# The first iteration of each FFN reordered by chunks of columns, with the norm of later chunks behind it

## Chip, cores, metric

One NeuronCore of a Trainium2 chip. The metric is the device time in microseconds of one execution; lower is better.

## What is computed

One inference step of a two-layer decoder for 1024 prompt tokens and 8 x 4 sample tokens, model width 1024, all in float32. Each layer is a token mixer followed by a SwiGLU FFN; the change touches only the FFNs.

```python
def rmsnorm(x, g):
    xf = xf * lax.rsqrt(jnp.mean(xf * xf, axis=-1, keepdims=True) + RMS_EPS)
    return xf.astype(x.dtype) * g
def swiglu(h, w_in, w_out):
    g, u = jnp.split(h @ w_in, 2, axis=-1)
    return (jax.nn.silu(g) * u) @ w_out
# per sub-layer, shift, scale and gate from the conditioning vector
h = rmsnorm(x, norm_g[i, 1]) * (1 + sc) + sh
x = x + gt * swiglu(h, ffn_w_in[i], ffn_w_out[i])
```

D_FF is 2816. The 32 sample tokens have a shift, scale and gate for each sequence of the batch.

## The kernel before

The activations lie transposed in SBUF: `xT` has 8 tiles (KD) of 128 features by 1056 tokens (T). The tokens are cut into NCH = 3 chunks of CH = 352 columns; the last one ends with the 32 sample tokens. A float32 product is made of three matmuls: every operand is split into a rounded high half and a low half, and hi x hi, lo x hi and hi x lo are added in PSUM.

`ffn_phase` (L639) runs N = 11 iterations. Each takes two blocks of 128 gate and up columns (`a` = 0 and 1) and the two matching blocks of the down weights (`a` = 2). The weights of an iteration are three loads of 1 MB into the two halves of `raw` (blocks 0 and 2 share half 0). ACT writes the high half (`split_hi`, L687), POOL the low one (`split_lo`, L711). PE then makes, for block 0 and every chunk, gate and up products (48 matmuls, L740 to L742), the same for block 1, and then the down products of every chunk (48 matmuls, L760 to L762). For each gate tile ACT computes Silu (L694), and DVE multiplies with up, copies the high half and subtracts for the low half (L780, L782, L784). DVE adds each down tile times the gate to `xT` (`residual_add`, L80; two short operations more for the sample tokens).

`SplitNorm` (L213) makes h. For each chunk: ACT squares 8 tiles (L248) into a ring of three; DVE (chunk 0) or POOL (chunks 1 and 2) adds them (L257, L260); one PE matmul with ones sums over partitions (`pe_sums`, L268); DVE scales to the variance (L315), ACT takes the root (L282), DVE the reciprocal (L320). For each of the 8 tiles DVE multiplies x by scale and rstd (L345) into a ring of three, ACT adds the shift and rounds for h_hi (L292), and DVE subtracts for h_lo (L349). The sample columns have three products of their own ahead of chunk 2 (L327 to L331) and a subtraction behind it (L355).

Each engine works through its own instructions in order and waits on semaphores; the order is written out by hand. POOL: sums of chunk 1, low half of block 0, sums of chunk 2, low half of block 1, then block 2. `pe_chunk` puts the sum of chunk ch + 1 ahead of the wait for chunk ch's tiles. In the first iteration PE goes through block 0 for the three chunks, then block 1 for the three, then the down products; DVE does the whole norm (`dve_all`) ahead of the first gate. PSUM banks 0 to 5 take gate and up of chunk ch in 2ch and 2ch + 1, and down tile q in q % 6; banks 5, 6 and 7 also take the norm's three sums.

Of the kernel before, what the change touches and what calls it, by code (L numbers as in the profile page):

```python
# [27 lines left out]
NB = 8  # L28
# [184 lines left out]
class SplitNorm:  # L213
# [96 lines left out]
    def dve_all(self, dve):  # L310
        c, m = self.c, self.m

        def variance(ch):
            dve.wait_ge(self.sum_ready, ch + 1)
            dve.tensor_scalar(self.rstd[:, ch * CH:(ch + 1) * CH], c.ps[:, 5 + ch, 0:CH], 1.0 / D, EPS, ALU.mult, ALU.add).then_inc(self.var_ready, 1)  # L315

        def invert(ch):
            dve.wait_ge(self.std_ready, ch + 1)
            r = self.rstd[:, ch * CH:(ch + 1) * CH]
            dve.reciprocal(r, r).then_inc(self.rstd_ready, 1)  # L320
            dve.wait_ge(self.rstd_ready, ch + 1)

        def sample():

            hs = self.hs[:]
            hb = hs.rearrange("p k (b t) -> p k b t", t=NT)
            dve.tensor_tensor(hs, c.xT[:, :, SEQ:T], self.rstd[:, SEQ:T].unsqueeze(1).to_broadcast([P, KD, NS]), ALU.mult).then_inc(self.s_step, 1)  # L327
            dve.wait_ge(self.s_step, 1)
            dve.tensor_tensor(hb, hb, m[:, KD:2 * KD, 1:1 + NB].unsqueeze(3).to_broadcast([P, KD, NB, NT]), ALU.mult).then_inc(self.s_step, 1)
            dve.wait_ge(self.s_step, 2)  # L330
            dve.tensor_tensor(hb, hb, m[:, 0:KD, 1:1 + NB].unsqueeze(3).to_broadcast([P, KD, NB, NT]), ALU.add).then_inc(self.s_ready, 1)  # L331

        self.add_squares(dve, 0)
        variance(0)
        invert(0)
        for ch in range(NCH):
            w = self.cols(ch)
            if ch == 2:
                sample()
            for j in range(KD + 2):  # L340
                n = ch * KD + j
                if j < KD:
                    if n >= self.SQ:
                        dve.wait_ge(self.lo_ready, n - self.SQ + 1)
                    dve.scalar_tensor_tensor(out=self.g[:, n % self.SQ, 0:w.stop - w.start], in0=c.xT[:, j, w], scalar=m[:, KD + j, 0:1],  # L345
                                             in1=self.rstd[:, w], op0=ALU.mult, op1=ALU.mult).then_inc(self.g_ready, 1)
                if j >= 2:
                    dve.wait_ge(self.hi_ready, n - 1)
                    dve.scalar_tensor_tensor(out=self.hlo[:, j - 2, w], in0=self.g[:, (n - 2) % self.SQ, 0:w.stop - w.start], scalar=m[:, j - 2, 0:1],  # L349
                                             in1=self.hhi[:, j - 2, w].bitcast(F32), op0=ALU.add, op1=ALU.subtract).then_inc(self.lo_ready, 1)  # L350
            if ch < 2:
                variance(ch + 1)
                invert(ch + 1)
# [3 lines left out]
        dve.wait_ge(self.s_lo, 1)  # L357

# [280 lines left out]
def ffn_phase(nc, c, d, layer):  # L639
# [3 lines left out]
    with ExitStack() as ctx:  # L643
# [14 lines left out]
        src = d.ffn[layer]  # L658
        block = ctx.enter_context(nc.Block())

        @block.sync
        def _(sp):

            sp.dma_start(raw[:, 0, :], src[0]).then_inc(raw_ready[0], 16)
            sp.dma_start(raw[:, 1, :], src[1]).then_inc(raw_ready[1], 16)
            sp.wait_ge(w_lo, 1)
            sp.dma_start(raw[:, 0, :], src[2]).then_inc(raw_ready[0], 16)
            with sp.Fori(0, N - 1) as i:
                for a in range(3):
# [8 lines left out]
        def _(act):  # L678
# [29 lines left out]
        def _(pool):  # L708
# [1274 lines left out]
```

## Time and profile before

| | |
|---|---|
| median of 3 runs | 2947.04 us (2945.07 to 2947.34) |
| profiled execution, its own time | 2950.77 us |
| its span, first to last instruction | 2949.1 us |
| PE busy | 2378.6 us, 81% |
| PE weight loads | 2210.3 us, 75% |
| DVE busy | 1403.1 us, 48% |
| ACT busy | 691.8 us, 23% |
| POOL busy | 772.9 us, 26% |
| mean granted clock of TensorE | 0.90 of full |

The busy shares are means over stages of very different kind: front, FFN 0 (168.6 to 949 us), projection, attention, output projection, FFN 1 (2109.4 to 2889 us), final norm. Read each stage by its own waits. Idle time of an engine that isn't the bottleneck costs nothing.

### The profile page before, as it was taken

The page shows a single profiled execution, that of the slowest core. Times are in us where ns is not written, and L with a number is a line of the kernel's source. Part 1 is how long each engine was busy: PE and PEld are TensorE (multiplying, and loading weights), DVE is VectorE, ACT ScalarE, POOL GpSimd, SP SyncE. Part 2 cuts the span into 40 slices and gives each one's busy share as a digit, 9 for nine tenths or more (in the row PEclk, how much of TensorE's full clock was granted, in tenths as well). Part 3 has the DMA queues.
Part 4 walks back from the last instruction along what each step waited for, and adds up shares of the span by engine and source line. Part 5 has one row for each costly group of instructions (what it writes and reads, how often), then busy time and mean ns, then how long its engine had stood idle before and what let it go on. Part 6 is the DMA issues. An engine that isn't in the chain of part 4 may idle for free. (4 is left out here: it accounts for less than half of the span.)

```text
span 2949.1 us, 41660 instructions
## 1 busy us (share of the span) xinstructions
PE 2378.6 (81%) x15217; PEld 2210.3 (75%) x15217; DVE 1403.1 (48%) x2994; ACT 691.8 (23%) x1144; POOL 772.9 (26%) x594
## 2 busy tenths in 40 slices
PE   3659999999999499784313789568689999999995
PEld 2649999999999399643212567337689999999994
DVE  6664333333333810289996678223463333333336
ACT  2232111111110422240002888312231111111101
POOL 3432112211120345400001677522231122111210
PEclk8779999999999699886655999788899999999997
DMA  8421111111110344542211110581111111111101
GB/s 357 180 122 69 46 43 43 53 46 43 43 43 0 112 150 161 138 115 80 68 51 32 39 30 15 174 287 57 44 43 44 43 43 51 63 43 43 43 14 59
DMA packets 85772, 230.74 MB, mean 78 GB/s; under 512 B 14516, under 2 KB 50868, under 8 KB 71604
## 3 DMA queue, kind: packets, MB, share of 16 engines
q1 hardware_dynamic: 73264, 205.33, 19.8%
q0 software_dynamic: 10480, 23.85, 2.6%
q8 instruction: 54, 0.88, 0.1%
q10 hardware_dynamic: 1940, 0.40, 0.1%
q14 instruction: 34, 0.28, 0.0%
HBM read 200.77 MB, written 28.76 MB: 78 GB/s over the span
## 5 line engine op out<-in xcount | busy, mean ns | idle before, releaser
L740 PE MATMUL ps<-f_hhi,f_whi 128*128 128x352 f32 x2112 | 687.8, 326 | 31.4 <-DVE f_hlo L349 17.3
L741 PE MATMUL ps<-f_hhi,f_wlo 128*128 128x352 f32 x2112 | 682.0, 323 | 0.0
L742 PE MATMUL ps<-f_hlo,f_whi 128*128 128x352 f32 x2112 | 681.0, 322 | 0.0
L711 POOL TENSOR_TENSOR f_wlo<-f_raw,f_whi 128x2048 fp32r<-128x2048 f32 x66 | 303.9, 4605 | 1108.8 <-ACT f_whi L687 1108.8
L80 DVE SCALAR_TENSOR_TENSOR xT<-ps,mod,xT 128x352 f32<-128x352 f32 (+1 forms) x576 | 327.9, 573 | 213.6 <-PE ps L762 121.4
L740 PEld LDWEIGHTS ps<-f_hhi,f_whi 128*128 128x128 f32 x2112 | 400.5, 190 | 35.1 <-DVE f_hlo L349 35.1
L741 PEld LDWEIGHTS ps<-f_hhi,f_wlo 128*128 128x128 f32 x2112 | 401.5, 190 | 0.0
L742 PEld LDWEIGHTS ps<-f_hlo,f_whi 128*128 128x128 f32 x2112 | 400.3, 190 | 0.0
L760 PE MATMUL ps<-f_ahi,f_whi 128*128 128x352 f32 x1056 | 340.6, 323 | 0.0
L761 PE MATMUL ps<-f_ahi,f_wlo 128*128 128x352 f32 x1056 | 338.3, 320 | 0.0
L762 PE MATMUL ps<-f_alo,f_whi 128*128 128x352 f32 x1056 | 338.0, 320 | 0.0
L687 ACT ACTIVATE f_whi<-f_raw 128x2048 fp32r<-128x2048 f32 x66 | 126.4, 1915 | 554.2 <-PE ps L762 418.2
L1460 POOL TENSOR_TENSOR pa_pr<-pa_pr,pa_rl 128x128 f32<-128x128 f32 (+7 forms) x128 | 142.8, 1147 | 367.9 <-DVE pa_rl L1440 367.8
L780 DVE TENSOR_TENSOR f0n_g<-f0n_sq,ps 128x352 f32<-128x352 f32 x66 | 34.4, 521 | 399.2 <-PE ps L742 396.8
L780 DVE TENSOR_TENSOR f1n_g<-f1n_sq,ps 128x352 f32<-128x352 f32 x66 | 34.4, 521 | 398.1 <-PE ps L742 395.7
L761 PEld LDWEIGHTS ps<-f_ahi,f_wlo 128*128 128x128 f32 x1056 | 198.4, 188 | 0.0
L760 PEld LDWEIGHTS ps<-f_ahi,f_whi 128*128 128x128 f32 x1056 | 198.0, 188 | 0.0
L762 PEld LDWEIGHTS ps<-f_alo,f_whi 128*128 128x128 f32 x1056 | 197.9, 187 | 0.0
L940 PE MATMUL ps<-pj_hhi,pj_whi 128*128 128x352 f32 x408 | 135.3, 332 | 18.3 <-DVE pj_hlo L355 10.3
L1131 PE MATMUL ps<-ix_part,rowsum 128*128 128x1 f32 x64 | 16.3, 324 | 155.7 <-DVE ix_rel L1229 155.6
L1432 DVE TENSOR_TENSOR pa_ptlo<-ps,pa_pthi 128x512 fp32r<-128x512 f32 x144 | 97.7, 689 | 79.5 <-ACT pa_pthi L1494 78.3
L1380 PE MATMUL ps<-kst,pa_qst 128*128 128x512 f32 (+3 forms) x192 | 75.2, 391 | 73.7 <-DMA pa_qst<-halves 41.5
(322 smaller groups left out, 3828.4 us busy)
## 6 DMA issues: line engine op xcount, KB each, us to landing
f_raw<-in_ffn SPq DMA_DIRECT2D x66, 1024.0 KB, 4.7
ada_raw<-in_ada SPq DMA_DIRECT2D x18, 2048.0 KB, 11.9
sa_kv<-in_ckv POOLq DMA_DIRECT2D x54, 256.0 KB, 4.4
ix_vT<-in_ada SPq DMA_DIRECT2D x12, 1024.0 KB, 5.1
sa_kv<-in_ckv SPq DMA_DIRECT2D x42, 256.0 KB, 4.6
pj_raw<-in_win SPq DMA_DIRECT2D x9, 1024.0 KB, 5.6
pa_qst<-halves SPq DMA_DIRECT2D x128, 64.0 KB, 2.3
halves<-pj_shi SPq DMA_DIRECT2D x45, 176.0 KB, 1.8
```

The source lines that it names most:

```text
L80: ins = dve.scalar_tensor_tensor(out=x, in0=psum[:, 0:n], scalar=gate[:, 0:1], in1=x, op0=ALU.mult, op1=ALU.add)
L687: act.activation(whi[:, a, :], raw[:, a % 2, :], ACT.Copy).then_inc(w_hi, 1)
L711: pool.tensor_tensor(wlo[:, a, :], raw[:, a % 2, :], whi[:, a, :].bitcast(F32), ALU.subtract).then_inc(w_lo, 1)
L740: pe.matmul(c.ps[:, bank, 0:CH], hi[:, k, side, :], hhi[:, k, col], start=(k == 0), stop=False)
L741: pe.matmul(c.ps[:, bank, 0:CH], lo[:, k, side, :], hhi[:, k, col], start=False, stop=False)
L742: last = pe.matmul(c.ps[:, bank, 0:CH], hi[:, k, side, :], hlo[:, k, col], start=False, stop=(k == KD - 1))
L760: pe.matmul(c.ps[:, q % 6, 0:CH], hi[:, k, w], ahi[:, k, col], start=(k == 0), stop=False)
L761: pe.matmul(c.ps[:, q % 6, 0:CH], lo[:, k, w], ahi[:, k, col], start=False, stop=False)
L762: last = pe.matmul(c.ps[:, q % 6, 0:CH], hi[:, k, w], alo[:, k, col], start=False, stop=(k == 1))
L940: pe.matmul(c.ps[:, q, 0:CH], hi[:, k, w], hhi[:, k, col], start=(k == 0), stop=False)
L1432: dve.tensor_tensor(ptlo[:, t % 3, :], c.ps[:, 4 + t % 2, :], pthi[:, t % 3, :].bitcast(F32), ALU.subtract).then_inc(lo_ready, 1)
L1460: pool.tensor_tensor(p, p, rl[:, i % 3, g:g + 1].to_broadcast([P, (q + 1) * P]), ALU.mult).then_inc(p_ready, 1)
```

## The change

The norm's DVE part is cut into methods, and `dve_tiles` can run other DVE work after each tile (`between`). In the first iteration PE goes by chunks: both blocks of gate and up of chunk 0, block 0 of chunk 1, the down products of chunk 0, block 1 of chunk 1, both of chunk 2, the down products of chunks 1 and 2. The sum of the next chunk now comes after the gate side of block 0. Unit n of gate and up uses banks 2(n % 3) and the next. The ring of squares and the ring of g are busy with the norm, so the first iteration's Silu and gated tiles go into half 1 of `raw` (`sg0`, `af0`). The orders on ACT, POOL, DVE and SP are written anew for it; later iterations are unchanged. Helpers cut here: `first_down` and `first_gate_up` hold the same matmuls as `iteration`.

```diff
--- before.py
+++ after.py
@@ -307,54 +307,58 @@
...
+    def dve_tiles(self, dve, ch, between=lambda j: None):
+        m, w = self.m, self.cols(ch)
+        for j in range(KD + 2):
+            n = ch * KD + j
+            if j < KD:
+                if n >= self.SQ:
+                    dve.wait_ge(self.lo_ready, n - self.SQ + 1)
+                dve.scalar_tensor_tensor(out=self.g[:, n % self.SQ, 0:w.stop - w.start], in0=self.c.xT[:, j, w], scalar=m[:, KD + j, 0:1],
+                                         in1=self.rstd[:, w], op0=ALU.mult, op1=ALU.mult).then_inc(self.g_ready, 1)
+            if j >= 2:
+                dve.wait_ge(self.hi_ready, n - 1)
+                dve.scalar_tensor_tensor(out=self.hlo[:, j - 2, w], in0=self.g[:, (n - 2) % self.SQ, 0:w.stop - w.start], scalar=m[:, j - 2, 0:1],
+                                         in1=self.hhi[:, j - 2, w].bitcast(F32), op0=ALU.add, op1=ALU.subtract).then_inc(self.lo_ready, 1)
+            between(j)
+
...
@@ -656,6 +660,9 @@
+        sg0, af0 = [raw[:, 1, i * 2 * CH:(i + 1) * 2 * CH].rearrange("p (a n) -> p a n", a=2) for i in range(2)]
@@ -665,7 +672,13 @@
             sp.dma_start(raw[:, 1, :], src[1]).then_inc(raw_ready[1], 16)
             sp.wait_ge(w_lo, 1)
             sp.dma_start(raw[:, 0, :], src[2]).then_inc(raw_ready[0], 16)
-            with sp.Fori(0, N - 1) as i:
+            sp.wait_ge(w_lo, 3)
+            sp.dma_start(raw[:, 0, :], src[3]).then_inc(raw_ready[0], 16)
+            sp.wait_ge(a_ready, 6)
+            sp.dma_start(raw[:, 1, :], src[4]).then_inc(raw_ready[1], 16)
+            sp.wait_ge(w_lo, 4)
+            sp.dma_start(raw[:, 0, :], src[5]).then_inc(raw_ready[0], 16)
+            with sp.Fori(1, N - 1) as i:
...
@@ -693,9 +706,48 @@
                         act.wait_ge(gated, i * 6 + (a * NCH + ch - 1))
                     act.activation(sg[:, (a * NCH + ch) % 2, :], c.ps[:, 2 * ch, 0:CH], ACT.Silu).then_inc(silu_ready, 1)
-            norm.act_all(act, lambda a: split_hi(a, 0, True))
+            def first_silu(n):
+                act.wait_ge(gate_ready, n + 1)
+                if n >= 2:
+                    act.wait_ge(gated, n - 1)
+                act.activation(sg0[:, n % 2, :], c.ps[:, 2 * (n % 3), 0:CH], ACT.Silu).then_inc(silu_ready, 1)
+            def split_hi_second(a):
+                act.wait_ge(raw_ready[a % 2], raw_count(a, 1))
+                if a < 2:
+                    act.wait_ge(up_ready, 5 + a)
+                else:
+                    act.wait_ge(down_ready, GD)
...
+            norm.act_squares(act, 0, 8)
+            split_hi(0, 0, True)
+            norm.act_std(act, 0)
+            split_hi(1, 0, True)
+            norm.act_squares(act, 8, 11)
+            for j in range(KD):
+                norm.act_hi(act, j, j + 1)
+                if 11 + j < 16:
+                    norm.act_squares(act, 11 + j, 12 + j)
+            norm.act_std(act, 1)
             split_hi(2, 0, True)
-            with act.Fori(0, N - 1) as i:
+            for j in range(KD):
+                norm.act_hi(act, 8 + j, 9 + j)
+                norm.act_squares(act, 16 + j, 17 + j)
+            act.wait_ge(w_lo, 2)
+            first_silu(0)
+            first_silu(1)
+            norm.act_std(act, 2)
+            norm.act_hi(act, 16, 18)
+            first_silu(2)
+            norm.act_hi(act, 18, 24)
+            first_silu(3)
+            first_silu(4)
+            split_hi_second(0)
+            first_silu(5)
+            split_hi_second(1)
+            split_hi_second(2)
+            with act.Fori(1, N - 1) as i:
                 silus(0, i)
                 split_hi(0, i + 1)
                 silus(1, i)
@@ -709,8 +761,11 @@
             def split_lo(a, n):
                 pool.wait_ge(w_hi, n + 1)
                 pool.tensor_tensor(wlo[:, a, :], raw[:, a % 2, :], whi[:, a, :].bitcast(F32), ALU.subtract).then_inc(w_lo, 1)
-            norm.pool_all(pool, lambda a: split_lo(a, a))
+            split_lo(0, 0)
+            norm.add_squares(pool, 1)
+            split_lo(1, 1)
             split_lo(2, 2)
+            norm.add_squares(pool, 2)
             with pool.Fori(1, N) as i:
...
                     split_lo(a, 3 * i + a)
@@ -719,18 +774,60 @@
         def _(pe):
             norm.pe_sums(pe, 0)
-            def iteration(i, first):
...
+            def first_gate_up(n):
+                ch, a = divmod(n, 2)
...
+                pe.wait_ge(w_lo, a + 1)
+                for side in range(2):
+                    bank = 2 * (n % 3) + side
+                    if n == 3:
+                        pe.wait_ge(added, 7 + side)
+                    for k in range(KD):
+                        if a == 0 and side == 0:
+                            pe.wait_ge(norm.lo_ready, KD * ch + (k + 1 if ch == 0 else KD))
+                            if ch == 2:
+                                pe.wait_ge(norm.s_lo, 1)
...
+                    last.then_inc(up_ready if side else gate_ready, 1)
+                    if a == 0 and side == 0 and ch < 2:
+                        norm.pe_sums(pe, ch + 1)
+            def first_down(ch):
...
+                pe.wait_ge(w_lo, 3)
+                pe.wait_ge(a_ready, 2 * (ch + 1))
+                for m in range(KD):
+                    q = ch * KD + m
+                    if q in (6, 7) or q >= 14:
+                        pe.wait_ge(added, q - 5)
+                    else:
+                        pe.wait_ge(gated if q % 2 else silu_ready, (1, 2, 3, 0, 5, 6, 4)[q // 2])
...
+                    last.then_inc(down_ready, 1)
+            def iteration(i):
                 for a in range(2):
                     pe.wait_ge(w_lo, 3 * i + (a + 1))
...
                     for ch in range(NCH):
...
-                        if a == 0 and first:
-                            norm.pe_chunk(pe, ch)
                         for side in range(2):
                             bank = 2 * ch + side
-                            if a == 0 and not first:
+                            if a == 0:
                                 pe.wait_ge(added, i * GD + (bank - 5))
                             if a == 1 and side == 0:
                                 pe.wait_ge(silu_ready, i * 6 + (ch + 1))
@@ -761,15 +858,69 @@
...
                         last.then_inc(down_ready, 1)
-            iteration(0, True)
+            first_gate_up(0)
+            first_gate_up(1)
+            first_gate_up(2)
+            first_down(0)
+            first_gate_up(3)
+            first_gate_up(4)
+            first_gate_up(5)
+            first_down(1)
+            first_down(2)
             with pe.Fori(1, N) as i:
-                iteration(i, False)
+                iteration(i)
         @block.vector
         def _(dve):
-            norm.dve_all(dve)
-
-            with dve.Fori(0, N) as i:
+            def first_gate(n):
+                ch, a = divmod(n, 2)
+                s, col = af0[:, n % 2, :], slice(ch * CH, (ch + 1) * CH)
+                dve.wait_ge(silu_ready, n + 1)
+                dve.wait_ge(up_ready, n + 1)
+                dve.tensor_tensor(s, sg0[:, n % 2, :], c.ps[:, 2 * (n % 3) + 1, 0:CH], ALU.mult).then_inc(gated, 1)
+                dve.wait_ge(gated, n + 1)
+                dve.tensor_copy(ahi[:, a, col], s).then_inc(a_step, 1)
+                dve.wait_ge(a_step, n + 1)
+                dve.tensor_tensor(alo[:, a, col], s, ahi[:, a, col].bitcast(F32), ALU.subtract).then_inc(a_ready, 1)
+                if n >= 1:
+                    dve.wait_ge(a_ready, n)
+            def first_residual(q):
+                ch, m = divmod(q, KD)
+                dve.wait_ge(down_ready, q + 1)
+                if q >= 1 and ch == 2:
+                    dve.wait_ge(added, q)
+                residual_add(dve, c, c.ps[:, q % 6, 0:CH], m, ch, 2 * layer + 1, tmp[:], (rstep, m + 1), added)
+            def between(j):
+                if j == 3:
+                    first_gate(2)
+                elif j >= 4:
+                    first_residual(j - 4)
+            norm.add_squares(dve, 0)
+            norm.dve_variance(dve, 0)
+            norm.dve_invert(dve, 0)
+            norm.dve_tiles(dve, 0)
+            norm.dve_variance(dve, 1)
+            norm.dve_invert(dve, 1)
+            norm.dve_tiles(dve, 1)
+            first_gate(0)
+            first_gate(1)
+            norm.dve_variance(dve, 2)
+            norm.dve_invert(dve, 2)
+            norm.dve_sample(dve)
+            norm.dve_tiles(dve, 2, between)
+            norm.dve_sample_lo(dve)
+            first_residual(6)
+            first_residual(7)
+            first_gate(3)
+            first_gate(4)
+            first_gate(5)
+            for q in range(KD, GD):
+                first_residual(q)
+            with dve.Fori(1, N) as i:
                 for a in range(2):
                     for ch in range(NCH):
                         q = a * NCH + ch
```

## Rows read from the trace of the kernel before

**Rows 1.** Windows of layer 0's FFN, each engine's busy time, clock, DMA.
```profile
193.20:225.80 32.60, 21.33 (x99) 20.22 (x99) 30.83 (x41) 16.60 (x29) 11.92 (x8) 0.76 0.00 1
...
282.00:350.60 68.60, 68.60 (x433) 68.60 (x432) 24.17 (x58) 9.83 (x10) 13.80 (x3) 1.00 0.13 47
```

**Rows 2.** PE's waits from 165 to 310 us for h_lo: total, times, longest.
```profile
PE ps L740 <- DVE f_hlo L349: 8.7, 2, 5.4
```

**Rows 3.** PE's timeline, first iteration of layer 0, then of layer 1.
```profile
193.26 0.66 PE L740 MATMUL ps<-f_hhi,f_whi 128*128 128x352 f32 x1 [5.42 <-DVE f_hlo L349]
...
204.61 0.86 PE L268 MATMUL ps<-f0n_rstd,ones 128*128 128x352 f32 x2 [1.52 <-POOL f0n_rstd L260]
...
208.72 0.66 PE L740 MATMUL ps<-f_hhi,f_whi 128*128 128x352 f32 x1 [3.25 <-DVE f_hlo L349]
...
225.79 0.63 PE L740 MATMUL ps<-f_hhi,f_whi 128*128 128x352 f32 x1 [6.45 <-DVE f_hlo L355]
...
231.50 0.39 PE L741 MATMUL ps<-f_hhi,f_wlo 128*128 128x352 f32 x1
...
281.95 0.32 PE L740 MATMUL ps<-f_hhi,f_whi 128*128 128x352 f32 x1
...
2167.13 0.63 PE L740 MATMUL ps<-f_hhi,f_whi 128*128 128x352 f32 x1 [7.65 <-DVE f_hlo L355]
...
2170.20 0.43 PE L741 MATMUL ps<-f_hhi,f_wlo 128*128 128x352 f32 x1
```

**Rows 4.** DVE's timeline, first iteration of layer 0.
```profile
176.58 2.35 DVE L320 RECIPROCAL f0n_rstd<-f0n_rstd 128x352 f32<-128x352 f32 x1 [0.56 <-ACT f0n_rstd L282]
...
178.97 2.92 DVE L345 SCALAR_TENSOR_TENSOR f0n_g<-xT,mod,f0n_rstd 128x352 f32<-128x352 f32 x3
...
181.82 4.81 DVE L349 SCALAR_TENSOR_TENSOR f_hlo<-f0n_g,mod,f_hhi 128x352 fp32r<-128x352 f32 x1
...
193.12 0.52 DVE L315 TENSOR_SCALAR f0n_rstd<-ps 128x352 f32<-128x352 f32 x1
...
196.59 2.51 DVE L345 SCALAR_TENSOR_TENSOR f0n_g<-xT,mod,f0n_rstd 128x352 f32<-128x352 f32 x3
...
208.58 0.52 DVE L315 TENSOR_SCALAR f0n_rstd<-ps 128x352 f32<-128x352 f32 x1
...
212.05 4.31 DVE L327 TENSOR_TENSOR f0n_hs<-xT,f0n_rstd 128x256 f32<-128x256 f32 x1
...
217.20 1.47 DVE L345 SCALAR_TENSOR_TENSOR f0n_g<-xT,mod,f0n_rstd 128x320 f32<-128x320 f32 x3
...
225.22 0.42 DVE L355 TENSOR_TENSOR f_hlo<-f0n_hs,f_hhi 128x256 fp32r<-128x256 f32 x1
...
231.63 0.51 DVE L780 TENSOR_TENSOR f0n_g<-f0n_sq,ps 128x352 f32<-128x352 f32 x1
...
263.08 0.58 DVE L80 SCALAR_TENSOR_TENSOR xT<-ps,mod,xT 128x352 f32<-128x352 f32 x1 [0.37 <-PE ps L762]
```

**Rows 5.** POOL's timeline there.
```profile
181.47 4.77 POOL L711 TENSOR_TENSOR f_wlo<-f_raw,f_whi 128x2048 fp32r<-128x2048 f32 x1
...
199.69 4.86 POOL L260 TENSOR_TENSOR f0n_rstd<-f0n_rstd,f0n_sq 128x352 f32<-128x352 f32 x4 [1.47 <-ACT f0n_sq L248]
...
211.50 4.57 POOL L711 TENSOR_TENSOR f_wlo<-f_raw,f_whi 128x2048 fp32r<-128x2048 f32 x1 [6.95 <-ACT f_whi L687]
```

**Rows 6.** DMA issues: first load of layer 0, second of layer 1; us to landing.
```profile
f_raw<-in_ffn SPq DMA_DIRECT2D x1, 1024.0 KB, 4.7
...
f_raw<-in_ffn SPq DMA_DIRECT2D x1, 1024.0 KB, 6.8
```

**Rows 7.** ACT's timeline there: a weight split, the Silu table load.
```profile
178.42 1.90 ACT L687 ACTIVATE f_whi<-f_raw 128x2048 fp32r<-128x2048 f32 x1
...
226.34 1.28 ACT L694 ACT_TABLE_LOAD   x1
...
227.63 0.82 ACT L694 ACTIVATE f0n_sq<-ps 128x352 f32<-128x352 f32 x2
```

More of the change, by code:

```diff
@@ L308, in act_all @@
         self.act_hi(act, 16, 24)
[L310 to L353, printed above, removed]
@@ new lines, in dve_variance, with dve_invert, dve_sample @@
+    def dve_variance(self, dve, ch):
+        dve.wait_ge(self.sum_ready, ch + 1)
+        dve.tensor_scalar(self.rstd[:, ch * CH:(ch + 1) * CH], self.c.ps[:, 5 + ch, 0:CH], 1.0 / D, EPS, ALU.mult, ALU.add).then_inc(self.var_ready, 1)
+    def dve_invert(self, dve, ch):
+        dve.wait_ge(self.std_ready, ch + 1)
+        r = self.rstd[:, ch * CH:(ch + 1) * CH]
+        dve.reciprocal(r, r).then_inc(self.rstd_ready, 1)
+        dve.wait_ge(self.rstd_ready, ch + 1)
+    def dve_sample(self, dve):
+        c, m, hs = self.c, self.m, self.hs[:]
+        hb = hs.rearrange("p k (b t) -> p k b t", t=NT)
+        dve.tensor_tensor(hs, c.xT[:, :, SEQ:T], self.rstd[:, SEQ:T].unsqueeze(1).to_broadcast([P, KD, NS]), ALU.mult).then_inc(self.s_step, 1)
+        dve.wait_ge(self.s_step, 1)
+        dve.tensor_tensor(hb, hb, m[:, KD:2 * KD, 1:1 + NB].unsqueeze(3).to_broadcast([P, KD, NB, NT]), ALU.mult).then_inc(self.s_step, 1)
+        dve.wait_ge(self.s_step, 2)
+        dve.tensor_tensor(hb, hb, m[:, 0:KD, 1:1 + NB].unsqueeze(3).to_broadcast([P, KD, NB, NT]), ALU.add).then_inc(self.s_ready, 1)
@@ L354, in dve_all, with dve_sample_lo @@
+    def dve_sample_lo(self, dve):
         dve.wait_ge(self.s_hi, 1)
@@ L357, in dve_all @@
         dve.wait_ge(self.s_lo, 1)
+    def dve_tiles(self, dve, ch, between=lambda j: None):
[12 more added lines that the diff above has]
+            between(j)
+    def dve_all(self, dve):
+        self.add_squares(dve, 0)
+        self.dve_variance(dve, 0)
+        self.dve_invert(dve, 0)
+        for ch in range(NCH):
+            if ch == 2:
+                self.dve_sample(dve)
+            self.dve_tiles(dve, ch)
+            if ch < 2:
+                self.dve_variance(dve, ch + 1)
+                self.dve_invert(dve, ch + 1)
+        self.dve_sample_lo(dve)
     def pool_all(self, pool, split_weights):
@@ L694, in silus @@
                     act.activation(sg[:, (a * NCH + ch) % 2, :], c.ps[:, 2 * ch, 0:CH], ACT.Silu).then_inc(silu_ready, 1)
-            norm.act_all(act, lambda a: split_hi(a, 0, True))
-            split_hi(2, 0, True)
-            with act.Fori(0, N - 1) as i:
+            def first_silu(n):
[9 more added lines that the diff above has]
+                    act.wait_ge(down_ready, GD)
+                act.activation(whi[:, a, :], raw[:, a % 2, :], ACT.Copy).then_inc(w_hi, 1)
+            norm.act_squares(act, 0, 8)
[8 more added lines that the diff above has]
+            norm.act_std(act, 1)
+            split_hi(2, 0, True)
+            for j in range(KD):
[15 more added lines that the diff above has]
+            with act.Fori(1, N - 1) as i:
                 silus(0, i)
@@ L720, in _, with weights @@
             norm.pe_sums(pe, 0)
-            def iteration(i, first):
+            def weights(a):
+                k = dict(k=KD, s=2) if a < 2 else dict(k=2)
+                form = "p (k s m) -> p k s m" if a < 2 else "p (k m) -> p k m"
+                return whi[:, a, :].rearrange(form, **k), wlo[:, a, :].rearrange(form, **k)
+            def first_gate_up(n):
+                ch, a = divmod(n, 2)
+                hi, lo = weights(a)
+                col = slice(ch * CH, (ch + 1) * CH)
+                pe.wait_ge(w_lo, a + 1)
[6 more added lines that the diff above has]
+                            pe.wait_ge(norm.lo_ready, KD * ch + (k + 1 if ch == 0 else KD))
+                            if ch == 2:
+                                pe.wait_ge(norm.s_lo, 1)
+                        pe.matmul(c.ps[:, bank, 0:CH], hi[:, k, side, :], hhi[:, k, col], start=(k == 0), stop=False)
+                        pe.matmul(c.ps[:, bank, 0:CH], lo[:, k, side, :], hhi[:, k, col], start=False, stop=False)
+                        last = pe.matmul(c.ps[:, bank, 0:CH], hi[:, k, side, :], hlo[:, k, col], start=False, stop=(k == KD - 1))
+                    last.then_inc(up_ready if side else gate_ready, 1)
+                    if a == 0 and side == 0 and ch < 2:
+                        norm.pe_sums(pe, ch + 1)
@@ new lines, in first_down @@
+            def first_down(ch):
+                hi, lo = weights(2)
+                col = slice(ch * CH, (ch + 1) * CH)
+                pe.wait_ge(w_lo, 3)
[6 more added lines that the diff above has]
+                        pe.wait_ge(gated if q % 2 else silu_ready, (1, 2, 3, 0, 5, 6, 4)[q // 2])
+                    w = slice(m * P, (m + 1) * P)
+                    for k in range(2):
+                        pe.matmul(c.ps[:, q % 6, 0:CH], hi[:, k, w], ahi[:, k, col], start=(k == 0), stop=False)
+                        pe.matmul(c.ps[:, q % 6, 0:CH], lo[:, k, w], ahi[:, k, col], start=False, stop=False)
+                        last = pe.matmul(c.ps[:, q % 6, 0:CH], hi[:, k, w], alo[:, k, col], start=False, stop=(k == 1))
+                    last.then_inc(down_ready, 1)
```

## The prediction

> **What bounds it now.** I read the busy table first, then the stretches, the waits and the timelines of TensorE (PE), VectorE (DVE), ScalarE (ACT) and GpSimd (POOL). From the 282nd microsecond to the end of an FFN, PE is never idle: 433 matmuls fill 68.6 us at a granted clock of 1.00, so no other engine can lengthen those iterations [rows 1]. The first iteration of each FFN is different. Before it and inside it PE waits for the norm: 8.7 us in two waits for tiles of h_lo (the longest 5.4, before the first matmul) [rows 2] and 6.45 us for the sample columns [rows 3]. In the stretch from 193.2 to 225.8 PE has 21.3 us of work in 32.6 us at a clock of 0.76, while DVE is busy for 30.8 us [rows 1]. So there the bound is DVE's chain: PE starts at 193.26, restarts at 208.72 and 225.79, each time 0.1 us after DVE's last tile, and reaches the second iteration at 281.95 [rows 3]. A change here is worth what it does to the last restart plus what PE still has to do after it. I call 48 matmuls (one unit of gate and up for one chunk, or the down products of one chunk) a unit; 432 matmuls are 9 units, 68.6 us, so a unit is 7.63 us at the high clock, 0.159 us a matmul.
>
> **Two prices of rows.** First, DVE operations that read two tensors in SBUF stand still while a POOL operation runs. The 0.58 us h_lo tile that started at 181.82, 0.35 us after POOL's 4.77 us weight split, took 4.81 us and ended 0.4 us after it; the first sample product took 4.31 us beside the next split, and the two of the same size behind it 0.43 [rows 4, 5]. A reciprocal, with one tensor, keeps 2.35 us beside POOL's sums, and a residual, whose other operand lies in PSUM, 0.58 [rows 4]. Beside POOL's sums of squares (four in 4.86 us) DVE gets one operation through per POOL operation, 1.2 us instead of 0.55. The Trainium skill (SBUF — State Buffer, "Who interferes with whom") states the same exclusive port for two SBUF inputs, and adds that the order of issue decides who blocks. By it a DVE operation issued first would hold POOL and lose nothing itself, 4.4 us less at each hold that falls that way; the traces show the split winning every time. Second, after a wait PE runs at the lower of its two levels (1.2 of 2.4 GHz): from 225.79 twenty matmuls go at 0.293 us, to 231.5; from 2167.13 ten do [rows 3]. I take 16 for each new restart, 2.15 us, bounds 1.35 and 2.7.
>
> **The change, DVE's chain in layer 0.** Times are positions in the old trace's clock.
> - Split of weights 0: raw data land 4.7 us after the issue at 168.63 [rows 6], 173.3. ACT's high half (1.90 us [rows 7]) moves ahead of the square root at 176.05 and ends at 175.25, so the root is not late. POOL splits from 175.3 to 179.9, mostly under DVE's reciprocal, which is not held. The first tile product, at 178.97 as before [rows 4], is held to 180.3.
> - Chunk 0: ACT now gives squares of chunk 1 one at a time between tiles, so POOL's seven sums stretch to 189.35, beside nine DVE operations: 9.45 us for 5.0. POOL then begins the second split (its high half needs raw data that land 6.8 us after the issue [rows 6], in time), and the next DVE operation is held 4.75 us, to 194.5. Five more end chunk 0 at about 197.15; before it was 193.2. PE can start on the first tile, at 183.9 instead of 193.26, but ends the gate side only with the last one.
> - The sum for chunk 1 now stands behind those 24 matmuls: three left, 0.88, and the sum at the low clock, 1.54. Chunk 1's variance starts at 199.7, not at 193.12 [rows 4]: 6.6 late.
> - Root, high half of the down weights, POOL's third split: the same order that gave the 4.31 us hold at 212.05, 3.47 us after its variance started at 208.58 [rows 4]. Now the hold falls on chunk 1's first tile: it ends 7.85 us after the variance, where before tiles were under way after 3.47; less 0.4 for its own work, 4.0 more, 10.6 late in all.
> - Chunk 1's tiles took 12.05 us from 196.59 with seven sums beside them; the same sums are now paced by ACT, I add 0.5: they end at 219.75. PE has done the second unit of chunk 0 by about 213 and waits 6.7 us.
> - Chunk 2's sum used to be done at 205.5, under the tiles [rows 3]. Now it follows the gate side of chunk 1: 24 matmuls with 16 slow, 3.8 + 2.15, then 0.86 and 0.1 of handover. Variance at 226.7 instead of 208.58 [rows 4], 18.1 late. The first two gates (1.45 us each, three operations from 231.63) fit in this hole after the Silu table load.
> - The sample product is no longer held: 3.9 back, 14.2 late.
> - Chunk 2's tiles took 8.4 us from 217.20 to 225.64 [rows 4]. Added among them: gate 2, 1.45, 0.35 of waiting for ACT's table load and Silu before it, residuals 0 to 5 at 0.55, and residual 6, 0.6, because the fourth unit of gate and up goes into bank 0 (it waits for seven residuals). That is 5.7, so 19.9 late: PE restarts at 245.7.
>
> **PE after the restart.** Then 7 units were left; now 5 are: two, 15.26 us, are taken out (the second unit of chunk 0 and its down products). End of the first iteration: 245.7 + 5 x 7.63 + 2.15 = 286.0, against 281.95: 4.1 us later. In layer 1 the front of the norm costs the same to 0.1 us, the restart comes 19.4 after 2167.13, and the old one paid only 1.5 us of low clock: 19.4 - 15.26 + 0.65 = 4.8 later. Residuals keep up in the last two down units (0.55 against 0.95 for six matmuls, as before).
>
> **Costed at nothing.** The four extra table switches (Silu, root, Silu again in each layer): one load is 1.28 us [rows 7]. The root's load lies under the wait for the variance, the first Silu's under PE's gate side; of the second Silu's, 0.35 is in the sum, and without the three tile products in front it would be 1.75. The Trainium skill (ScalarE: Activation LUTs, "What ACT_TABLE_LOAD costs") puts 1.38 us of drain beside each load; the row shows the Silu right behind it with none, and by the page the result would be some 2.8 us later for both layers. SP's load of the second gate weights now waits for all six gates, as their scratch lies in that buffer: about 275 + 5 to land + 1.9 + 4.6 = 286, and PE wants it at 286 + 22.9, so 22 us of cover; the wait before it on SP also holds the load of the down weights, needed at about 332. The loads that went out earlier find an empty queue. Projection and final phase keep their order, and the unrolled code adds no work.
>
> **Sum.** Profiled execution 2950.77 us (span 2949.1): +4.1 + 4.8 = 2959.7. Against the median of the runs shown, which is 3.7 lower, 2947.04 + 8.9 = 2955.9. Bounds of a layer: low-clock matmuls 10 or 20, three places (the sum of chunk 1 at 0.86 or 1.54 too), -2.3 to +1.1; holds beside the paced sums, from nothing to the full 1.2 us on each, -4 to +2; tables 0 to +1.4. Both layers err together: about -8 to +7 around the sum.
>
> **Rivals.** (a) The forecast: VectorE's chain stays the bound and grows more than PE's remainder shrinks. For it: DVE is 95% busy in that stretch already and gets seven residuals and three gates more ahead of the restart. (b) The clock stays up. PE has matmuls from 183.9 on; if no stretch counts as idle, the gate side costs 3.8, the sum 0.86, the restart nothing: 5 us less a layer, 2946, no measurable change. Against it: the gap ahead of 208.72 held a sum (204.61), and 20 matmuls after it were slow all the same [rows 3]. Part of this, or lighter holds, leads to the same result. (c) Faster, by one mechanism: POOL does not win the shared port in the new order, that is, DVE's operations are mostly in first. All holds of a layer are 0.8 + 4.4 + 4.4 + 4.0 + 3.5 = 17 us; without them PE would be the bound in chunk 0 and restart near 227, 14 us less a layer, 2919. It decides once over 7.5 of the 17 us are gone (result beyond -5.9). Against it: three norms show the same 4.8 us hold. (d) Slower still: each Silu and root switch lands on DVE's chain, 1.3 to 2.7 a layer more, 2958 to 2961. (e) That the next iteration waits for weights is out by the 22 us above.
>
> **Chances.** A measurement of this kernel can't tell under 0.2%, 5.9 us, from no change. (a) with (d) 0.62, slower by over 5.9; (b) and the weak end of (a) 0.26, within it; (c) and what leads towards it 0.12. The likeliest case alone spans 2951 to 2963. Eight in ten: down to 2943, between (b) and a third of (c)'s gain, and up to 2965, the upper bounds together.
>
> **What would show it.** Right: first matmul of the first iteration near 184, chunk 1's variance near 200, a hold over 4 us inside chunk 0's and on chunk 1's first tile, PE idle 5 to 8 us before chunk 1 and some 5 us before the fourth unit, and the second iteration 4 to 5 us later. Wrong: that fourth unit before 241, or PE without idle after chunk 0; then the holds or the clock were mispriced. It would also fall if Identity asked for a table of its own after Silu.

## The result, and the profile after

The changed kernel takes 2958.34 us (median of 5 runs, 2951.46 to 2964.24) against 2947.04 (5 runs, 2944.81 to 2947.48): ratio 1.0041, 95% interval 1.0024 to 1.0057, slower by 11.3 us. Run again later it took 2959.08 (5 runs) against 2946.92, ratio 1.0040 (1.0026 to 1.0054). The profiled execution has a span of 2956.5 us.

Executions begin at slightly different times (the first square of FFN 0's norm stands at 168.64 before and at 164.88 after), so I count from a layer's first square. The table gives, for layer 0 and layer 1, when the variances of chunks 1 and 2 start on DVE, when PE goes on behind its last long wait (the last restart; after the change it is the start of the fourth unit), and when its second iteration begins.

| | variance 1 | variance 2 | last restart | second iteration |
|---|---|---|---|---|
| before | 24.5, 25.0 | 39.9, 40.5 | 57.2, 57.7 | 113.3, 112.8 |
| after | 31.7, 31.5 | 58.6, 59.5 | 76.9, 77.9 | 118.1, 118.1 |

So the FFNs lose 4.8 and 5.3 us, 10.0 of the 11.3. In the second profile of the changed kernel the numbers are 31.7, 58.7, 77.1, 118.2 and 31.5, 59.5, 77.8, 117.8. The rest is not placed. The stretch from layer 0's second iteration to layer 1's first square, in which PE's work is the same in both kernels, took 1827.4 us before, 1828.7 and 1832.3 in the two profiles after, and the profiles of the experiments lie between 1826.4 and 1831.0. The span of the profiled pair grows by 7.4 us only, because its front, too, was 3.8 us longer before (168.64 against 164.88).

In layer 0, from the first square to the second iteration, before and then after (length, then the busy time of PE, PEld, DVE, ACT and POOL, the granted clock and DMA):

```profile
168.64:281.95 113.31, 80.56 (x439) 77.37 (x439) 76.63 (x119) 38.94 (x64) 37.23 (x19) 0.80 0.15 56
...
164.88:282.94 118.06, 82.73 (x439) 77.59 (x440) 78.95 (x109) 40.76 (x66) 37.80 (x19) 0.80 0.15 54
```

Of the 4.75 us, PE is idle for 2.6 more (35.3 for 32.7) and busy for 2.2 more with the same 439 matmul records.

VectorE in layer 0 of the changed kernel. These rows answer to [rows 4]:

```profile
175.21 3.76 DVE L342 SCALAR_TENSOR_TENSOR f0n_g<-xT,mod,f0n_rstd 128x352 f32<-128x352 f32 x3
...
181.23 1.25 DVE L346 SCALAR_TENSOR_TENSOR f_hlo<-f0n_g,mod,f_hhi 128x352 fp32r<-128x352 f32 x1
...
186.42 4.82 DVE L346 SCALAR_TENSOR_TENSOR f_hlo<-f0n_g,mod,f_hhi 128x352 fp32r<-128x352 f32 x1
...
196.62 0.52 DVE L312 TENSOR_SCALAR f0n_rstd<-ps 128x352 f32<-128x352 f32 x1 [3.28 <-PE ps L268]
...
200.10 5.44 DVE L342 SCALAR_TENSOR_TENSOR f0n_g<-xT,mod,f0n_rstd 128x352 f32<-128x352 f32 x3
...
223.47 0.53 DVE L312 TENSOR_SCALAR f0n_rstd<-ps 128x352 f32<-128x352 f32 x1 [3.62 <-PE ps L268]
...
226.95 0.42 DVE L323 TENSOR_TENSOR f0n_hs<-xT,f0n_rstd 128x256 f32<-128x256 f32 x1
...
231.62 0.52 DVE L880 TENSOR_TENSOR f_raw<-f_raw,ps 128x352 f32<-128x352 f32 x1 [0.43 <-ACT f_raw L713]
...
241.08 1.07 DVE L80 SCALAR_TENSOR_TENSOR xT<-ps,mod,xT 128x352 f32<-128x352 f32 x2
```

The first three tile products take 3.76 us (the first takes 1.43 of them, beside the end of POOL's first split), those beside POOL's sums go at 1.2 us each, the h_lo tile at 186.42 is held for 4.82, and the first of the three at 200.10 again, for 4.45 of the 5.44. The two variances wait 3.28 and 3.62 us for PE. The sample product is free of the hold, 0.42 instead of 4.31. POOL's splits, beside [rows 5]. The second and third begin 0.35 and 0.53 us ahead of the operation that is held; the first runs under variance and reciprocal, and ends 1.0 us after the first tile product began:

```profile
171.74 4.51 POOL L763 TENSOR_TENSOR f_wlo<-f_raw,f_whi 128x2048 fp32r<-128x2048 f32 x1 [40.45 <-ACT f_whi L700]
...
186.07 4.78 POOL L763 TENSOR_TENSOR f_wlo<-f_raw,f_whi 128x2048 fp32r<-128x2048 f32 x1
...
199.57 4.60 POOL L763 TENSOR_TENSOR f_wlo<-f_raw,f_whi 128x2048 fp32r<-128x2048 f32 x1 [8.72 <-ACT f_whi L700]
```

PE, beside [rows 3]:

```profile
180.28 0.63 PE L796 MATMUL ps<-f_hhi,f_whi 128*128 128x352 f32 x1 [8.59 <-DVE f_hlo L346]
...
191.29 0.66 PE L796 MATMUL ps<-f_hhi,f_whi 128*128 128x352 f32 x1 [4.67 <-DVE f_hlo L346]
...
195.21 1.38 PE L268 MATMUL ps<-f0n_rstd,ones 128*128 128x352 f32 x2
...
217.24 0.63 PE L796 MATMUL ps<-f_hhi,f_whi 128*128 128x352 f32 x1 [9.18 <-DVE f_hlo L346]
...
220.31 0.39 PE L797 MATMUL ps<-f_hhi,f_wlo 128*128 128x352 f32 x1
...
222.61 0.75 PE L268 MATMUL ps<-f0n_rstd,ones 128*128 128x352 f32 x2
...
241.81 0.63 PE L796 MATMUL ps<-f_hhi,f_whi 128*128 128x352 f32 x1 [4.61 <-DVE xT L80]
...
282.94 0.32 PE L837 MATMUL ps<-f_hhi,f_whi 128*128 128x352 f32 x1
```

It starts at 180.28, 15.4 us behind the first square and not 24.6; the last tile of chunk 0 lets it end the gate side at 195.21. Then it waits 9.18 us for chunk 1, runs 11 matmuls at the low clock (217.24 to 220.31, both counted, as in all such counts here), sums for chunk 2 at 222.61 and stands 4.61 us before the fourth unit. PE's waits in that stretch, total, times, longest, beside [rows 2]:

```profile
PE ps L796 <- DVE f_hlo L346: 23.9, 5, 9.2
...
PE ps L796 <- DVE xT L80: 4.6, 1, 4.6
```

PE now waits 23.9 us in five pieces, before 8.7 in two and 6.45. That is not all a loss, because before it also stood in front of the sum for chunk 1, ahead of its first tile:

```profile
186.30 1.54 PE L268 MATMUL ps<-f0n_rstd,ones 128*128 128x352 f32 x2 [10.85 <-POOL f_wlo L711]
```

ACT, beside [rows 7]: the first split waits only 1.00 us for its data, and the Silu of gate 2 follows its table load at once.

```profile
169.74 1.91 ACT L700 ACTIVATE f_whi<-f_raw 128x2048 fp32r<-128x2048 f32 x1 [1.00 <-DMA f_raw<-in_ffn]
...
229.83 1.28 ACT L713 ACT_TABLE_LOAD   x1
...
231.13 0.46 ACT L713 ACTIVATE f_raw<-ps 128x352 f32<-128x352 f32 x1
```

### The profile page after: what moved, and what is told of

It reads as the page before. It is cut to its first block and busy times, and to the rows that moved or that the text cites. A ratio compares the mean times of both kernels' runs of the same rounds, so it can differ in the third digit from the quotient of the medians.

```text
span 2956.5 us, 41548 instructions
## 1 busy us (share of the span) xinstructions
PE 2380.7 (81%) x15217; PEld 2209.4 (75%) x15217; DVE 1421.7 (48%) x2994; ACT 672.4 (23%) x1130; POOL 774.9 (26%) x594
## 5 line engine op out<-in xcount | busy, mean ns | idle before, releaser
L837 PE MATMUL ps<-f_hhi,f_whi 128*128 128x352 f32 x1920 | 619.2, 323 | 0.0
L838 PE MATMUL ps<-f_hhi,f_wlo 128*128 128x352 f32 x1920 | 615.2, 320 | 0.0
L839 PE MATMUL ps<-f_hlo,f_whi 128*128 128x352 f32 x1920 | 614.9, 320 | 0.0
L838 PEld LDWEIGHTS ps<-f_hhi,f_wlo 128*128 128x128 f32 x1920 | 360.7, 188 | 0.0
L837 PEld LDWEIGHTS ps<-f_hhi,f_whi 128*128 128x128 f32 x1920 | 360.1, 188 | 0.0
L839 PEld LDWEIGHTS ps<-f_hlo,f_whi 128*128 128x128 f32 x1920 | 359.9, 187 | 0.0
L857 PE MATMUL ps<-f_ahi,f_whi 128*128 128x352 f32 x960 | 309.6, 323 | 0.0
L858 PE MATMUL ps<-f_ahi,f_wlo 128*128 128x352 f32 x960 | 307.6, 320 | 0.0
L859 PE MATMUL ps<-f_alo,f_whi 128*128 128x352 f32 x960 | 307.3, 320 | 0.0
L858 PEld LDWEIGHTS ps<-f_ahi,f_wlo 128*128 128x128 f32 x960 | 180.3, 188 | 0.0
L1091 PE MATMUL ps<-pj_hhi,pj_whi 128*128 128x352 f32 x408 | 134.7, 330 | 19.2 <-DVE pj_hlo L331 11.3
```

What stands on the lines that cost most here:

```text
L837: pe.matmul(c.ps[:, bank, 0:CH], hi[:, k, side, :], hhi[:, k, col], start=(k == 0), stop=False)
L838: pe.matmul(c.ps[:, bank, 0:CH], lo[:, k, side, :], hhi[:, k, col], start=False, stop=False)
L839: last = pe.matmul(c.ps[:, bank, 0:CH], hi[:, k, side, :], hlo[:, k, col], start=False, stop=(k == KD - 1))
L857: pe.matmul(c.ps[:, q % 6, 0:CH], hi[:, k, w], ahi[:, k, col], start=(k == 0), stop=False)
L858: pe.matmul(c.ps[:, q % 6, 0:CH], lo[:, k, w], ahi[:, k, col], start=False, stop=False)
L859: last = pe.matmul(c.ps[:, q % 6, 0:CH], hi[:, k, w], alo[:, k, col], start=False, stop=(k == 1))
```

## Experiments

Each is an edit of the changed kernel. The numbers in brackets are the start of the fourth unit (in the changed kernel the last restart) and the second iteration, layer 0 and layer 1, behind the first square; the changed kernel has (76.9, 77.9; 118.1, 118.1). A slow matmul is one that starts 0.29 us before the next and not 0.16; the one in which the clock rises counts as slow.

**Sums early.** The norm's sums on PE moved ahead of the gate side.

```diff
+                if a == 0 and ch < 2:
+                    norm.pe_sums(pe, ch + 1)
                 pe.wait_ge(w_lo, a + 1)
...
-                    if a == 0 and side == 0 and ch < 2:
-                        norm.pe_sums(pe, ch + 1)
```

> Only the place of the norm's sums on PE changes: the sum of chunk 1 stands ahead of the first gate side, that of chunk 2 ahead of the gate side of chunk 1, instead of behind them. If VectorE's chain is the bound, chunk 1's variance comes 3.3 us earlier (right behind chunk 0's last tile) and chunk 2's another 3.6 us earlier (right behind the two gates), so the restart of PE before the fourth unit and the second iteration come 6.9 us earlier in each layer, about 14 us in all: near 2944. If the loss lay in PE (its clock, its order), moving two short matmuls gains nothing: within 2 us of the changed kernel.

2943.85 us (10 runs) against 2947.73, ratio 0.9988 (0.9979 to 0.9998); (69.9, 70.5; 109.7, 111.4). The two variances on DVE:

```profile
192.07 0.52 DVE L312 TENSOR_SCALAR f0n_rstd<-ps 128x352 f32<-128x352 f32 x1
...
215.22 0.52 DVE L312 TENSOR_SCALAR f0n_rstd<-ps 128x352 f32<-128x352 f32 x1
```

Neither has an idle time in brackets any more: DVE gets each sum the moment it is free. The restart comes 7.1 and 7.4 us earlier for 6.9 expected, the second iteration 8.4 and 6.7. Where two short matmuls stand is worth more than the 4.8 and 5.3 us that the change lost.

**Splits moved.** POOL's second and third weight split go where DVE does variance and reciprocal.

```diff
             norm.add_squares(pool, 1)
+            pool.wait_ge(norm.lo_ready, KD)
             split_lo(1, 1)
-            split_lo(2, 2)
             norm.add_squares(pool, 2)
+            pool.wait_ge(a_ready, 2)
+            split_lo(2, 2)
```

> Only POOL's order changes: the second weight split waits for chunk 0's last tile, and the third goes behind the sums of chunk 2 and waits for the first two gates. Both then run while VectorE does variance and reciprocal. If the holds cost what the trace says, the 4.8 us tile in chunk 0 and the 5.4 us triple in chunk 1 fall to 0.6 and 1.5, 8.2 us a layer, 16 in all: near 2942. If the waits seen there were something else than POOL's weight split, they stay where they are and the time with them.

2942.51 us (10 runs) against 2947.73, ratio 0.9984 (0.9974 to 0.9993); (69.0, 68.8; 109.1, 109.7). DVE, the same tile that was held, the variance, the triple that was held:

```profile
188.43 0.57 DVE L346 SCALAR_TENSOR_TENSOR f_hlo<-f0n_g,mod,f_hhi 128x352 fp32r<-128x352 f32 x1
...
193.46 0.53 DVE L312 TENSOR_SCALAR f0n_rstd<-ps 128x352 f32<-128x352 f32 x1 [2.34 <-PE ps L268]
...
196.94 1.58 DVE L342 SCALAR_TENSOR_TENSOR f0n_g<-xT,mod,f0n_rstd 128x352 f32<-128x352 f32 x3
```

The tile of 4.82 us now takes 0.57 and the triple of 5.44 takes 1.58, 8.1 us less, and the restart is 7.9 and 9.1 us earlier for 8.2. So the holds were POOL's weight splits. That the restart moves by the same amount in layer 0 is in part chance: the first variance also waits less for PE (2.34 us for 3.28), and the second waits more (4.87 for 3.62), behind 20 slow matmuls and not 11.

**Free banks.** The fourth unit goes to banks 6 and 7.

```diff
-                    bank = 2 * (n % 3) + side
+                    bank = (6 if n == 3 else 2 * (n % 3)) + side
                     if n == 3:
-                        pe.wait_ge(added, 7 + side)
+                        pe.wait_ge(norm.var_ready, 3)
...
-                    if q in (6, 7) or q >= 14:
+                    if q in (6, 7) or q >= 12:
```

ACT's Silu and DVE's product read bank 6 and bank 7 for that unit.

> Only the banks of the fourth unit of gate and up change: 6 and 7, which the norm has left, instead of 0 and 1, so PE no longer waits for residuals 6 and 7, that stand behind all of chunk 2's tiles. If that wait is where the last restart is set, PE goes on right behind chunk 0's down products, 4.6 us earlier, and with no restart at the low clock: 1.6 to 2.7 more; 6 to 7 us a layer, 13 in all, near 2945. If PE's remaining work is bounded later by the tiles of chunk 2 anyway (they end 1.2 us before the old restart, but the unit after the next needs them), nothing is lost again. Rival: the fourth unit starts early, but the fifth waits, gain under 2 us.

2944.04 us (10 runs) against 2947.73, ratio 0.9989 (0.9979 to 0.9998); (72.1, 72.7; 110.3, 111.1). The last of PE's idle times in layer 0:

```profile
237.10 0.43 PE L816 MATMUL ps<-f_ahi,f_whi 128*128 128x352 f32 x1 [0.19 <-DVE xT L80]
```

Behind this 0.19 us there is none. The fourth unit starts 4.8 and 5.2 us earlier, the 20 and 13 slow matmuls that followed the restart are gone, and the second iteration comes 7.8 and 7.0 us earlier. The fifth unit did not wait.

**All three.**

> The three edits together. VectorE's chain is some 15 us shorter and no longer carries the restart; by the row durations the fourth unit starts 19 us earlier than in the changed kernel and the clock gives about 2 more: 21 us a layer, 42 in all, near 2917, faster than the kernel before by 1%. If the parts only uncover the same next wait, it stays within 3 us of the best of the three single edits.

2918.02 us (4 runs) against 2947.73, ratio 0.9897 (0.9880 to 0.9913): 1% faster than the kernel before; (59.1, 59.9; 97.3, 98.1), 20.7 and 20.0 us a layer less for 21. PE:

```profile
186.20 1.54 PE L268 MATMUL ps<-f0n_rstd,ones 128*128 128x352 f32 x2 [14.33 <-POOL f0n_rstd L260]
...
205.98 0.86 PE L268 MATMUL ps<-f0n_rstd,ones 128*128 128x352 f32 x2 [1.13 <-POOL f0n_rstd L260]
...
218.80 0.43 PE L818 MATMUL ps<-f_ahi,f_whi 128*128 128x352 f32 x1 [0.16 <-ACT f_raw L713]
...
221.72 0.43 PE L818 MATMUL ps<-f_ahi,f_whi 128*128 128x352 f32 x1 [0.73 <-DVE xT L80]
```

The 14.33 us ahead of the sum is now spent at the start, with tiles ready; after it PE has only idle times of 1.13 us and less (1.63 in layer 1).

**Chain only.** Sums early and splits moved, banks 0 and 1.

> The early sums and the moved splits together, banks 0 and 1 for the fourth unit as in the changed kernel, so VectorE's chain still sets the last restart. If both edits shorten that one chain, they add: 8.4 + 8.9 in layer 0 and 6.7 + 8.4 in layer 1, less 1.2 for the third split that now holds the first sample product: about 16 and 14 us against the changed kernel, near 2928. If they uncover PE or each other instead, the gain stays near 9 a layer, 2940.

2933.85 us (4 runs) against 2947.58, ratio 0.9957 (0.9940 to 0.9973); (64.0, 64.6; 105.0, 105.7): 13.0 and 12.4 us less. So they add on one chain, but 3.0 and 1.6 us short of what I wrote. In layer 0 the restarts of the two edits were 7.1 and 7.9 earlier, 15.0, and 12.9 was measured. Two holds are new: the sample product (1.57, not 0.42), which I had counted, and chunk 1's first triple, which I had not (2.68, where the moved splits alone had 1.58): variance 1 no longer waits for PE, so the second split (to 192.99) outlasts the reciprocal (to 191.65). 15.0 less the 2.25 us of both is 12.8. In layer 1 the same sum gives 14.2, and 13.2 was measured; that 1.0 is not placed. My 16 counted PE's clock behind the restart as well, where this kernel has 20 slow matmuls and the two had 13 and 14. DVE's held triple, its last variance and the held sample product:

```profile
191.69 2.68 DVE L342 SCALAR_TENSOR_TENSOR f0n_g<-xT,mod,f0n_rstd 128x352 f32<-128x352 f32 x3
...
208.64 0.52 DVE L312 TENSOR_SCALAR f0n_rstd<-ps 128x352 f32<-128x352 f32 x1
...
212.11 1.57 DVE L323 TENSOR_TENSOR f0n_hs<-xT,f0n_rstd 128x256 f32<-128x256 f32 x1
```

**First tiles early.** As all three, but the sum of chunk 1 stands behind the fifth k step of the first gate side.

```diff
+                        if n == 0 and side == 0 and k == 4:
+                            norm.pe_sums(pe, 1)
```

> The three edits of the combined kernel, but the sum of chunk 1 stands behind the fifth of the eight k steps of the first gate side rather than ahead of it. In the combined kernel PE is the bound from 187 on, and waits 14 us for POOL's sums with tiles ready from 180. Fifteen slow matmuls (4.4 us) now run before that wait ends; the clock is then still low, so of the 4.4 us about 3 to 4 come back: 3.5 us a layer, 7 in all, near 2911. If VectorE's chain still sets the end there, no change from 2918.

2917.91 us (4 runs) against 2947.58, ratio 0.9907 (0.9890 to 0.9925); (59.1, 59.8; 97.5, 97.9). What I expected did not come, and the other branch held: no change. PE starts the gate side 15.3 us behind the first square instead of 22.0, but then waits between tiles, 3.20 us ahead of the sum of chunk 2, and runs 13 slow matmuls behind it:

```profile
181.68 0.63 PE L800 MATMUL ps<-f_hhi,f_whi 128*128 128x352 f32 x1 [8.44 <-DVE f_hlo L346]
...
207.33 0.86 PE L268 MATMUL ps<-f0n_rstd,ones 128*128 128x352 f32 x2 [3.20 <-POOL f0n_rstd L260]
```

DVE's last tiles of chunk 1:

```profile
205.18 2.97 DVE L346 SCALAR_TENSOR_TENSOR f_hlo<-f0n_g,mod,f_hhi 128x352 fp32r<-128x352 f32 x3
```

They end at 208.15, the sum for chunk 2, which had waited for POOL, at 208.19, and chunk 1's gate side starts at 208.30, as far behind the first square as in the combined kernel (41.9 in both). Which of the two sets that start is not tested; both hang on DVE's tiles of chunk 1, as ACT's squares for POOL now go between them.

**Warm gap.** 48 matmuls into bank 7, thrown away, in the gap before chunk 1.

```diff
+                if n == 2:
+                    for side in range(2):
+                        for k in range(KD):
+                            pe.matmul(c.ps[:, 7, 0:CH], hi[:, k, side, :], hhi[:, k, 0:CH], start=(k == 0), stop=False)
...
```

> The changed kernel with 48 added matmuls whose result is thrown away (bank 7, before the sum of chunk 2 overwrites it), in the 9.2 us in which PE waits for chunk 1's tiles. The clock then should not have fallen when the gate side of chunk 1 begins. If the low clock there is on the chain, its 11 slow matmuls of layer 0 cost 11 x 0.134 = 1.5 us, and chunk 2's variance, the restart and the second iteration come 1.5 us earlier (116.5 behind the first square); layer 1 the same within a microsecond. If the clock does not matter or stays low all the same, 118.0 as before; if the added matmuls run over the end of the gap, later than that.

One execution: 2953.04 us against 2947.58; (75.3, 75.1; 115.6, 114.6).

```profile
218.51 0.43 PE L802 MATMUL ps<-f_hhi,f_whi 128*128 128x352 f32 x1 [1.36 <-DVE f_hlo L346]
...
222.45 0.75 PE L268 MATMUL ps<-f0n_rstd,ones 128*128 128x352 f32 x2
```

After 1.36 us of idle time the matmuls go at full rate, and 3.94 us pass to the sum instead of 5.37. The restart is 1.6 us earlier in layer 0 and 2.8 in layer 1, where 20 matmuls had been slow (20 x 0.134 = 2.7), not 11. The second iteration is 2.5 and 3.4 us earlier.

> The kernel with 48 thrown-away matmuls in PE's gap, timed. The one look gave 2.4 and 3.5 us less in the two layers where 1.5 was expected. If the surplus is the chance of where the clock rises behind the last restart, it changes from profile to profile while chunk 2's variance stays 1.6 us earlier than in the changed kernel; the sum over both layers is 3 to 6 us, near 2953.

2952.01 us (11 runs) against 2946.92, ratio 1.0014 (1.0005 to 1.0023), where the changed kernel beside it has 1.0040. Its landmarks repeat the first profile within 0.1 us, slow matmuls too (15 and 10 behind the restart both times). So in two profiles the surplus is not the chance that I had written it might be. It goes with fewer slow matmuls behind the restart, 15 and 10 for 20 and 13; why they are fewer is not shown.

**No switch for chunk 2's root.** ACT copies chunk 2's variance in both FFNs and the root is left out.

```diff
-            norm.act_std(act, 2)
+            act.activation(r2, r2, ACT.Copy).then_inc(norm.std_ready, 1)
```

> Leaves out the root of chunk 2's variance in both FFNs (ACT copies it instead), so ACT stays with Silu's table and two of the change's extra table loads in each layer are gone; everything else is the changed kernel. If loads lie under waits as the trace says, only the 0.43 us by which gate 2 waits for Silu goes, so the second iteration starts 117.6 us behind the norm's first square instead of 118.0. If each load also costs a drain of 1.4 us (the page of the Trainium skill on ScalarE, What ACT_TABLE_LOAD costs), it is 1.8 us or more earlier, 116.2 or less.

One execution, 2959.3 us against 2947.58; (76.5, 77.0; 116.3, 117.5). The restart is 0.42 us earlier in layer 0, which is the 0.43 by which gate 2 had waited. In layer 1 it is 0.87, of which 0.35 was already there at the variance. The second iteration in layer 0 is 1.7 earlier, close to what a drain would have given, but because 11 matmuls behind the restart were slow instead of 20. At the restart, ahead of that, the gain is 0.4 and 0.5 us and not 1.8, so no drain is on the chain.

**The changed kernel again.**

> The changed kernel once more, unedited, for a second profile and more times. By VectorE's chain the restart ahead of the fourth unit comes 76.9 us behind the norm's first square in both layers, to 0.2 us; the number of matmuls at the low clock behind it (20 in layer 0, 12 in layer 1) may differ, so the second iteration comes 117 to 118.5 us behind it. Time between 2951 and 2964.

2959.08 us; (77.1, 77.8; 118.2, 117.8), as expected but for layer 1's restart. 76.9 for both had left out the 20 slow matmuls at layer 1's chunk 1.

## Why the prediction was right

- **VectorE's chain sets the last restart.** Shown: two edits that shorten it move the restart by about what they take off (7.1 and 7.4 us, 7.9 and 9.1), and the third, which unties the fourth unit from it, gains the wait and the clock.
- **Holds by POOL.** Forecast 4.75 us inside chunk 0 and over 4 us on chunk 1's first tile; the rows have 4.82 and 4.45. Variance 1 was put at 31.1 behind the first square, it came at 31.7.
- **Sum behind the gate side.** Variance 2 was put at 58.1 and came at 58.6 and 59.5. In layer 0 two errors partly cancel in that: chunk 1's gate side began at 52.4, where I had 51.1 (PE waited 9.18 us for it, where I had 6.7 and had named 5 to 8 as the sign), but then 11 matmuls were slow, where I had 16. In layer 1 there were 20.
- **Gate 2 and residuals.** 0.35 us of waiting for Silu was 0.43. The restart was put at 77.1 in both layers and came at 76.9 and 77.9. Here too layer 0 is nearer than its parts: variance 2 was 0.5 late, and from it to the restart I had 19.0 us where 18.3 were measured.
- **PE after the restart.** Two units less, 5 left, with 16 slow matmuls assumed, 20 and 13 found. The second iteration was put 4.1 and 4.8 us later, it was 4.8 and 5.3. (In the kernel before, layer 1 had eleven slow matmuls behind 2167.13 and not ten; the 1.5 us that I took for them fits eleven.) In layer 1 the restart is 0.9 us later than in layer 0; that comes from the clock at chunk 1's gate side, 20 slow matmuls there and 11 in layer 0.
- **Sum.** Forecast +8.9, the two layers give +10.0, the medians of the two comparisons +11.3 and +12.2. The 1 to 2 us beyond the layers are not placed by any run. The mechanism was right, step by step; that the size came this near owes something to errors that cancelled.
- **The clock as a rival.** A clock that stays up would have made it no change. It did not stay up: 11 and 20 slow matmuls at chunk 1, 20 and 13 behind the restart. Filling one of its gaps gives 2.5 and 3.4 us at the second iteration, and the kernel stays slower.
- **The port as a rival.** It was no help: POOL's split won at each of the holds. The Trainium skill's page (SBUF — State Buffer, "Who interferes with whom") agrees with the holds of two-tensor operations (4.82 us for a tile of 0.57). Its clause on the order of issue is not at odds with them either, since the splits had begun 0.35 and 0.53 us before the operations that they held; a VectorE operation that was in first and held a split does not occur in these rows.
- **Tables.** The Trainium skill (ScalarE: Activation LUTs, "What ACT_TABLE_LOAD costs") puts a drain beside each table load. It does not show on the chain here: taking two loads away gave 0.4 and 0.5 us. And what I said of "the four extra table switches" holds for the first iterations alone. Before, ScalarE loaded Silu's table anew in ten iterations of each FFN, 20 times in all; after the change it is 4 times, all in the first iterations. That gave no time back: in FFN 0, from the second iteration to 949 us, PE is busy for all of the 667.05 us before, and after the change for all of the 667.06 us to 950.

There was cover enough: in the combined kernel the norm of chunks 1 and 2 lies behind PE's work but for waits of 1.63 us and less, once the sum for chunk 1 is done. In the changed kernel it was spent because each sum waited for a gate side, two splits fell on tiles, and one unit of PE waited for bank 0.

## What to carry to other kernels

When work is put behind a slower chain, follow that chain's own inputs first: a short matmul that feeds it should stand ahead of the long run it is meant to cover. Put long GpSimd operations where VectorE does operations that the rows show free of the hold: here the variance from PSUM (0.53 us) and the reciprocal (2.35). One tensor in SBUF is not by itself a guarantee. In the kernel before, this cast of one SBUF tensor, 0.34 us elsewhere, took 2.47 and ended 0.2 us behind POOL's split (226.39 to 230.95):

```profile
228.68 2.47 DVE L782 CAST f_ahi<-f0n_g 128x352 fp32r<-128x352 f32 x1
```

Before ordering units by need, look for a bank that ties the next unit to the end of the chain.

## What the runs showed that was not expected

The number of slow matmuls behind a wait repeats from one profile of a kernel to the next, to within one: 20 or 21 and 13 behind the last restart in both profiles of the changed kernel, 11 or 12 and 19 or 20 at chunk 1, 15 and 10 twice in the warm kernel. But it does not belong to the place: without chunk 2's root, the restart came 0.42 us earlier, behind the same wait of 4.6 us, and 11 matmuls were slow there and not 20. Nor is it told by the length of the wait: 9.18 us led to 11 slow matmuls in layer 0 and, in this row, to 20 in layer 1.

```profile
2163.72 0.63 PE L796 MATMUL ps<-f_hhi,f_whi 128*128 128x352 f32 x1 [9.18 <-DVE f_hlo L346]
```

And POOL's splits for the second iteration now fall among the residuals of the sample columns, whose last step reads two SBUF tensors (0.19 us for 32 columns):

```profile
277.12 3.68 DVE L86 TENSOR_TENSOR xT<-xT,f_tmp 128x32 f32<-128x32 f32 x1
...
285.52 4.33 DVE L86 TENSOR_TENSOR xT<-xT,f_tmp 128x32 f32<-128x32 f32 x1
```

3.68 and 4.33 us, and PE does not wait for either: it has no idle time from 268 to 300.
